# Padding the rows of three operand tiles of a TensorE-bound kernel (pitch 2048 bytes to 2064, 2112 and 2080)

## The reference, cut to what matters

```
h += 0.5 * m[2] * swiglu(modulate(rmsnorm(h, g), m[0], m[1]), w_in, w_out)     # FFN, hidden width 2816
h += m[5] * mix_out(lru_scans(...), spatial_gating(...))                       # token mixing
h += 0.5 * m[8] * swiglu(modulate(rmsnorm(h, g), m[6], m[7]), w_in, w_out)     # FFN
# swiglu: gate, up = split(z @ w_in); (silu(gate) * up) @ w_out
# m = silu(c) @ w_ada + b_ada, nine vectors per layer
```

## Time and profile before

| | us |
|---|---|
| median of 2 runs | 1663.96 (1663.55 and 1664.37) |
| span of the profiled execution, first to last instruction | 1660.2 |
| TensorE busy with matmuls | 1597.4 (96% of the span) |
| TensorE busy with weight loads | 1314.9 (79%) |
| VectorE, ScalarE, GpSimd busy | 976.7 (59%), 630.2 (38%), 176.0 (11%) |
| mean granted TensorE clock | 0.994 of full speed |

### The profile page before, as it was taken

One profiled execution on the slowest core, in us unless ns is written; L12 is line 12 of the kernel. 1 busy time (PEld: TensorE's weight loads), 2 busy tenths in 40 slices (PEclk: granted clock), 3 DMA queues, 4 the chain that ended last, 5 costly groups with the idle time before them and its releaser, 6 DMA issues.

```text
span 1660.2 us, 24197 instructions
## 1 busy us (share of the span) xinstructions
PE 1597.4 (96%) x8838; PEld 1314.9 (79%) x8838; DVE 976.7 (59%) x1352; ACT 630.2 (38%) x838; POOL 176.0 (11%) x158
## 2 busy tenths in 40 slices
PE   5999999999999999999999999999999997799998
PEld 4788888887777787888888778888888765799997
DVE  6777777323698467773322367773332279855554
ACT  3322222222563354433422242323222257366752
POOL 0000000011343210000001110000001035310001
PEclk9999999999999999999999999999999999999999
DMA  9455555442313335553234325552234322555553
GB/s 372 148 187 184 181 190 174 147 157 101 102 64 123 144 118 178 184 177 101 92 124 159 132 92 189 186 174 93 100 125 155 126 90 89 187 183 188 177 203 114
DMA packets 84187, 249.48 MB, mean 150 GB/s; under 512 B 12704, under 2 KB 13856, under 8 KB 82976
## 3 DMA queue, kind: packets, MB, share of 16 engines
q1 hardware_dynamic: 84128, 248.71, 43.5%
HBM read 247.62 MB, written 1.05 MB: 150 GB/s over the span
## 4 chain that ended last, share of the span: by engine, by line
PE 86%; DVE 6%; issue 2%; ACT 2%; POOL 2%; DMA 1%; DVEq 0%; POOLq 0%; SPq 0%; ACTq 0%
PE bank L327 28%; PE bank L328 27%; PE bank L329 27%; DMA ada_raw<-ada_w 1%; PE bank L515 1%; DVE w_lo L745 1%; DVE ada_acc L899 1%; PE bank L347 1%; ACT z_hi L609 1%; POOL y_lo L1150 1%; DMA res<-x_t 0%; PE bank L382 0%; DVE w_hi L973 0%; PE bank L498 0%; PE bank L496 0%
## 5 line engine op out<-in xcount | busy, mean ns | idle before, releaser
L745 DVE TENSOR_TENSOR w_lo<-raw,w_hi 128x1024 fp32r<-128x1024 f32 x320 | 398.2, 1245 | 444.7 <-ACT w_hi L583 244.0
L327 PE MATMUL bank<-z_hi,w_hi 128*128 128x512 f32 (+1 forms) x1600 | 588.9, 368 | 10.7 <-DVE z_lo L820 7.5
L328 PE MATMUL bank<-z_lo,w_hi 128*128 128x512 f32 (+1 forms) x1600 | 579.5, 362 | 0.0
L329 PE MATMUL bank<-z_hi,w_lo 128*128 128x512 f32 (+1 forms) x1600 | 579.2, 362 | 0.0
L327 PEld LDWEIGHTS bank<-z_hi,w_hi 128*128 128x128 f32 x1600 | 302.8, 189 | 69.0 <-issue 15.9
L589 ACT ACTIVATE w_hi<-raw 128x1024 fp32r<-128x1024 f32 x176 | 186.5, 1060 | 438.3 <-PE bank L329 438.0
L328 PEld LDWEIGHTS bank<-z_lo,w_hi 128*128 128x128 f32 x1600 | 302.9, 189 | 47.3 <-issue 2.7
L329 PEld LDWEIGHTS bank<-z_hi,w_lo 128*128 128x128 f32 x1600 | 302.6, 189 | 47.0
L583 ACT ACTIVATE w_hi<-raw 128x1024 fp32r<-128x1024 f32 x120 | 127.0, 1059 | 348.4 <-PE bank L329 346.6
L327 PE MATMUL bank<-h_hi,w_hi 128*128 128x512 f32 (+1 forms) x704 | 256.7, 365 | 0.0
L329 PE MATMUL bank<-h_hi,w_lo 128*128 128x512 f32 (+1 forms) x704 | 256.6, 365 | 0.0
(11 more groups left out here) (127 smaller groups left out, 1073.4 us busy)
## 6 DMA issues: line engine op xcount, KB each, us to landing
raw<-weights SPq DMA_DIRECT2D x320, 512.0 KB, 3.2
ada_raw<-ada_w SPq DMA_DIRECT2D x176, 256.0 KB, 3.0
ada_z<-ada_w SPq DMA_DIRECT2D x20, 1024.0 KB, 5.8
ada_head<-head_w SPq DMA_DIRECT2D x8, 1024.0 KB, 20.2
res<-x_t SPq DMA_DIRECT2D x1, 2048.0 KB, 8.1
bd<-gate_w SPq DMA_DIRECT2D x4, 256.0 KB, 4.1
out<-res SPq DMA_DIRECT2D x4, 256.0 KB, 2.2
ws<-sgu_w SPq DMA_DIRECT2D x2, 256.0 KB, 4.2
```

The source lines that it names most:

```text
L327: pe.matmul(bank_ap, w_hi[:, r, c], rhs_hi, start=start, stop=False)
L328: pe.matmul(bank_ap, w_hi[:, r, c], rhs_lo, start=False, stop=False)
L329: return pe.matmul(bank_ap, w_lo[:, r, c], rhs_hi, start=False, stop=stop)
L745: dve.tensor_tensor(w_lo[:, r, :], raw[:, r, :], w_hi[:, r, :].bitcast(F32), ALU.subtract).then_inc(lo_ready, 1)
```

## The change

Three tiles get longer rows. The added columns at the end of each row are never written or read.

```diff
+Z_PAD = 4
+HI_PAD = 16
+LO_PAD = 8
...
-        z_hi = sb("z_hi", [P, KD, T], F32R)
+        z_hi = sb("z_hi", [P, KD, T + Z_PAD], F32R)
         z_lo = sb("z_lo", [P, KD, T], F32R)
...
-            h_hi = sb("h_hi", [P, KF, T], F32R, ffn_scope)
-            h_lo = sb("h_lo", [P, KF, T], F32R, ffn_scope)
+            h_hi = sb("h_hi", [P, KF, T + HI_PAD], F32R, ffn_scope)
+            h_lo = sb("h_lo", [P, KF, T + LO_PAD], F32R, ffn_scope)
```

## The result

| | before | after |
|---|---|---|
| median, us | 1663.96 | 1676.43 (1676.13 and 1676.73) |
| span of the profiled execution, us | 1660.2 | 1674.3 |
| TensorE busy with matmuls, us | 1597.4 | 1611.9 |
| mean granted clock | 0.994 | 0.995 |

The ratio is 1.0073 (95% interval 1.0044 to 1.0103): the change costs 0.7%, or 12.5 us. The forecast was 1658 us, 0.4% less than before. The sign was wrong.

What follows compares the result with a forecast made beforehand. TensorE was taken as the bound: number of matmuls times distance between starts, plus its standstills. Terms -5.3 + 1.8 - 2.8 + 0 = -6.3 us took the span from 1660.2 to 1653.9; forecast median 1658 us, range 1625 to 1690.

Steps and rivals of the forecast that it cites:

- z at 512 columns and the 144 with w streaming: 3696 matmuls at 512 columns: taken as 0 change, bounds -49.5 to +49.2 us.
- third rival: z's stream at 512 columns loses its settled distance as z_hi's offset changes each row: slower, 1678 or 1696 us; chance 0.19.
- first form: z at 512 columns stays at the transient's 231.8 ns, +19.0 us; with the other terms +14 us, 1678 us.
- dearer form: Rows not starting at a multiple of 64 bytes also cost 6.7 ns, in z_hi and h_lo: 1696 us; 0.09 for slower.
- Modulo 128 bytes, w stays at 0, z_lo at 0 and y at 64, since all move together: Addresses of w, z_lo and y: all move by 128 bytes, so no change expected there.
- h at 512: 1584 matmuls of h at 512 columns: mean of two alignments, 230.0 ns, -5.3 us.
- h at 256: 528 matmuls of h at 256 columns: mean of 113.3 and 120.0, 116.7 ns, +1.8 us.
- z at 256: z at 256 columns: 832 of 1248 matmuls read z_hi and go to 116.7 ns, -2.8 us.
- y unchanged: y's matmuls: alignment kept at 64 modulo 128 bytes, distance to stay at 233.3 ns at 512 columns.
- Writers, waits, clock: Writers of padded tiles, TensorE's waits between stages and granted clock: as before, taken as 0; z_hi's writers at most 1.6 us.
- rival 2: Weight load and matmul reads of SBUF meet less, distances fall: -54 us, 1610 us, half of it 1637; chance 0.27.
- rival 1: Matmul distance goes with the stage, not the row's address, so time stays at 1664 us; chance 0.14.

Runs made afterwards that it cites:

- spacer128: Kernel before with a spare 128-byte tile between z_hi and z_lo, all pitches still 2048: 1671.27 us against its own before 1663.37, ratio 1.0043.
- probe2: Bare stream of products without the kernel's computation; offsets 128 to 480 bytes, other pitches, shifted w_lo: 226.7 ns at offset 256, 512 columns; z's changed-kernel addresses 232.5.
- z_pad128: Kernel before with only z_hi padded, by 128 bytes a row (pitch 2176): 1671.91 us against its own before 1663.85, ratio 1.0048.
- probe1: Kernel's computation left out, only products streamed, 36 cases of offsets 0 to 112 bytes and pitches: at 512 columns 226.7 ns at offset 0, 231.1 with hi pitch 2064.
- probe4: Bare stream without gaps between cases, 256 columns at offsets 192, 112 and 0 after six different streams: offset 192 took 113.3 or 117.8 ns, 112 took 113.3, 0 took 120.0.
- probe3: Bare stream of products with weight blocks of 128, 64 and 32 columns: at 512 columns and offset 0, 226.7, 230.0 and 231.7 ns.

## Why the prediction was wrong

**The step that failed** is "z at 512 columns and the 144 with w streaming ... I take 0". It measured +17.3 and +0.4 us, z going from 227.1 to 232.0 ns. I had no row for an offset of 16, 32 or 48 bytes and took the present 226.7 because it lay in the middle of the bounds. But it was no middle value: of all constant offsets tried on the chip it is the lowest at 512 columns (226.7 to 237.9), and none of the moves of z away from it won at that width. The trace of before hinted at it: its other rows at 512 columns were all longer, 233.3 for h and y and 231.8 for the same stream before it settled, and the lower bound, 213.3, was in no row. The last reading I gave to a rival.

**The third rival had the right number**, in its first form: 231.8 ns for z at 512 and 1678 us, against 232.0 and 1676.43. Its picture was not borne out, so that the two agree so closely is luck. It had the stream kept in its transient by an offset that changes at each row. But the changed kernel repeats one pattern in slot after slot (695 to 697 ns for the fifth row, 701 to 715 for the sixth), the bare stream of z's addresses stays at 232.5, and a changing offset is not needed: spacer128 loses 1.8 of the 4.9 ns with equal rows. The dearer form, 1696 us, did not happen.

**"Modulo 128 bytes, w stays at 0, z_lo at 0 and y at 64, since all move together"** was an assumption with two faults. The period is 256 bytes (probe2, z_pad128), and z_hi starts ahead of the 128 bytes that it adds, so its offset to w moved by 128. The prediction had no term for this; by itself it costs 1.8 ns at 512 columns (spacer128). The weights' address belongs in the sum: the offset that counts is relative (probe1).

**h at 512**: the mean of 226.7 and 233.3, 230.0, was taken; measured 231.3, so -3.2 us in place of -5.3. **h at 256**: 116.7 taken, 117.6 measured, +2.3 against +1.8. **z at 256**: 832 matmuls at 116.7 and 416 at 120.0 are 117.8 on average; measured 118.7, -1.5 against -2.8. These three interpolations hold in sign and roughly in size. That is partly luck: the trace showed the offsets 0 and 192 modulo 256, and h's were 192 + 64k and 64 + 32k.

**y unchanged**: right at 512 columns (233.4), wrong at 256 (117.8 for 113.5, +0.8 us), where it had the other of its two values (probe4).

**Writers, waits, clock**: as said. 633, 684 and 499 ns; no new wait; 0.995.

**The reads come apart** (rival 2) did not happen: no case at 512 columns went below 226.7 ns, with short loads or without. **Nothing happens** (rival 1) fell as well: with every other engine still, the stream at 512 columns took 226.7 to 237.9 ns by address alone. The Trainium skill ("TensorE: Matmul & The Clock Gate", Step-by-step: what each phase is for) says that loading the next weights takes nothing from the running matmul. The Trainium skill ("SBUF — State Buffer", Who interferes with whom) says that PE waits for no one. The measurement decides against what the prediction drew from the two, that no address matters. It does not show that the load takes something from the matmul (probe3 speaks against the simplest form of that). As to other engines this case agrees: the bare stream, with nothing beside it, has the same 226.7, 233.3, 120.0 and 113.3 ns as the kernel before.

The sum with the measured means, +16.1 us, stands to a span that grew by 14.1 and a median that grew by 12.5; so the accounting by distances is good to a few microseconds. The error of the sum was one term in the main, the 17.7 us of z and w past z at 512 columns that stood at 0. The range, 1625 to 1690, held the time, because it took in the rival.

## What to carry to other kernels

In a kernel that is bound by back-to-back matmuls, read the distance between starts for each pair of tiles, and look at the operands' addresses relative to each other modulo 256 bytes before touching them: a pad of 16 bytes a row on z_hi cost 0.8% here, a gap of 64 bytes ahead of h won 0.4%, and placing all of them won 1.1%. A pad of 256 bytes a row kept everything. When a term is large and the trace has no row for it, ask whether the present value is a typical one or the best one: if it is the best of what the trace shows, zero is not the middle.

## What the runs showed of the hardware

- Each matmul of a three-matmul fp32r product with 128 x 128 weights, with TensorE alone at full clock, takes 226.7 ns (offset 0) to 237.9 ns (offset 4 bytes) at 512 columns and 113.3 (112, or 192) to 120.0 ns (0, 80, 96) at 256. The order of the offsets is another at each width. At offset 0, 384 columns take 173.3 ns, and 128 columns take 111.7, hardly less than 256 at their best.
- The offset is the moving row's address less the weight block's, modulo 256 bytes. If w_lo lies 64 or 128 bytes off w_hi, 512 columns take 231.1 ns, at 32 bytes 233.3, at 256 again 226.7 (probe2, rows at 0).
- The stream settles. At 256 columns, offsets 0 and 112 settled to one distance behind each of six other streams; offset 192 settled to 113.3 or 117.8 ns, and offset 64 at 512 columns to 228.9 or 233.3. Other offsets were not tried in this way.
- Why an offset costs 13 to 25 ns over the 213.3 of streaming is not settled. At 512 columns it does not shrink with the weight load (190 or 108 ns long); no experiment here shows what it does go with.
